# Router copies, slot tables and norm factors placed elsewhere, and the last tail's roots taken together

## What is computed

```
x_lat = x_lat + mod_l[2] * o_lat                       # mixer, gated
h_lat = _modulate(_rmsnorm(x_lat, norm_ffn[l]), mod_l[3], mod_l[4])
...
g_logits = h @ w_group + b_group ; grp = argmax(g_logits)      # 4 groups
e_logits = (h @ w_expert + b_expert)[grp]                       # 8 experts of the group
top_p, top_i = top_k(softmax(e_logits), 2)
y = sum over the two experts of gate * (silu(x @ w1[e]) * (x @ w3[e])) @ w2[e]
x_lat = x_lat + mod_l[5] * y
...
return _rmsnorm(x_lat, final_norm)                     # then the second block starts with its own rmsnorm
```

## Time and profile before

| | |
|---|---|
| median of 3 runs | 2405.39 us (2403.98 to 2409.56) |
| the profiled execution, its own time | 2406.93 us |
| its span | 2405.6 us |
| TensorE busy (matmul) | 2192.5 us, 91% of the span |
| VectorE, ScalarE, GpSimd busy | 657.5, 357.0, 121.5 us |
| read from HBM, written | 589.84 MB, 21.23 MB |

### The profile page before, as it was taken

How to read it: one execution, slowest core, us unless ns; L and a number is a source line. 1 busy time by engine, 2 the same in 40 slices (tenths; PEclk the granted TensorE clock), 3 DMA queues, 4 the chain that set the end, 5 groups by cost and what they waited for, 6 DMA issues and landing times. The chain is left out here.

```text
span 2405.6 us, 27733 instructions
## 1 busy us (share of the span) xinstructions
PE 2192.5 (91%) x11542; PEld 1348.4 (56%) x11542; DVE 657.5 (27%) x1485; ACT 357.0 (15%) x831; POOL 121.5 (5%) x164
## 2 busy tenths in 40 slices
PE   6987998899999986999979999998599999989998
PEld 2454664656665543444555554544376458858873
DVE  2142332422222212313531111111355231034201
ACT  2052431200000001112520000000121122011000
POOL 4000000010000001000000000000110000000000
PEclk9988999899999998899989999999799999999999
DMA  9453163599999997621189999999644432443441
GB/s 331 143 216 136 56 260 149 209 414 420 420 420 420 421 420 295 225 71 67 50 322 415 420 419 420 419 420 418 229 142 134 133 112 97 158 140 119 153 152 41
DMA packets 154309, 601.75 MB, mean 250 GB/s; under 512 B 15289, under 2 KB 19073, under 8 KB 103488
## 3 DMA queue, kind: packets, MB, share of 16 engines
q1 hardware_dynamic: 144512, 582.98, 62.9%
q0 software_dynamic: 8144, 11.57, 1.5%
q10 hardware_dynamic: 1520, 5.32, 0.6%
HBM read 589.84 MB, written 21.23 MB: 254 GB/s over the span
## 5 line engine op out<-in xcount | busy, mean ns | idle before, releaser
L366 PE MATMUL psum<-ring,h_t 128*128 128x512 f32 (+1 forms) x1024 | 430.3, 582 | 4.5 <-ACT h_t L1072 2.1
L366 PEld LDWEIGHTS psum<-ring,h_t 128*128 128x128 f32 x1024 | 192.9, 193 | 234.8 <-issue 230.4
L399 PE MATMUL psum<-h_t,ring 128*128 128x256 f32 (+1 forms) x1424 | 311.7, 382 | 4.5 <-ACT ff_hid L2567 2.3
L399 PEld LDWEIGHTS psum<-h_t,ring 128*128 128x128 f32 (+1 forms) x1424 | 270.0, 190 | 45.9 <-issue 4.7
L2381 PE MATMUL psum<-ring,h_t 128*64 128x256 f32 x2272 | 262.1, 384 | 3.0 <-DMA ring<-in_expert_w_dram 2.1
L2381 PEld LDWEIGHTS psum<-ring,h_t 128*64 128x64 f32 x2272 | 158.0, 137 | 90.3 <-issue 11.8
L2381 PE MATMUL psum<-wide,h_t 128*64 128x256 f32 x1664 | 191.0, 382 | 2.3 <-DMA wide<-in_expert_w_dram 1.5
L2381 PEld LDWEIGHTS psum<-wide,h_t 128*64 128x64 f32 x1664 | 114.9, 137 | 66.6 <-issue 7.6
L337 DVE COPY h_t<-psum 128x512 f32<-128x512 f32 (+2 forms) x76 | 50.4, 663 | 319.6 <-PE psum L1933 294.5
L1933 PE MATMUL psum<-gates,h_row_tiles 128*128 128x256 f32 (+1 forms) x512 | 109.1, 370 | 5.6 <-DVE gates L1921 5.6
L1933 PEld LDWEIGHTS psum<-gates,h_row_tiles 128*128 128x128 f32 x512 | 89.9, 202 | 25.0 <-issue 12.2
(11 more groups left out here) (590 smaller groups left out, 2093.1 us busy)
## 6 DMA issues: line engine op xcount, KB each, us to landing
ring<-in_expert_w_dram SPq DMA_DIRECT2D x210, 1024.0 KB, 24.6
wide<-in_expert_w_dram SPq DMA_DIRECT2D x156, 1024.0 KB, 26.2
ring<-in_ada_w_dram SPq DMA_DIRECT2D x48, 1024.0 KB, 11.3
ring<-in_w_in_dram SPq DMA_DIRECT2D x30, 1024.0 KB, 5.1
ring<-in_diff_w_in_dram SPq DMA_DIRECT2D x12, 1024.0 KB, 15.7
gates<-in_expert_w_dram SPq DMA_DIRECT2D x12, 1024.0 KB
x<-in_expert_w_dram SPq DMA_DIRECT2D x12, 1024.0 KB, 27.8
ring<-in_w_gate_dram SPq DMA_DIRECT2D x12, 1024.0 KB, 4.9
```

The source lines that it names most:

```text
L366: mm = k.nc.tensor.matmul(banks[r][0:m, 0:nn], lhs(k0 + j, r), w[:, j, :], start=(k0 + j == 0), stop=(k0 + j == k_tiles - 1))
L399: mm = k.nc.tensor.matmul(banks[i][0:h, 0:n_rhs], w[:, j, b:b + h], rhs(k0 + j), start=(k0 + j == 0), stop=(k0 + j == k_tiles - 1))
```

## The change

Six edits, cut to their core:

```
 # second_tail: one root for both tiles, on [P, 2] instead of [P, 1] twice
-        def root(i):
+        def roots():
+            t_all, v2_all, r_all = ss[:, 0:T_LAT, 0], ss[:, 0:T_LAT, 1], ss[:, T_LAT:2 * T_LAT, 0]
             wait_for(dve, now(k.act_step, k.dve_step))
...
-        root(0)
         times_g(1)
-        r_at = reciprocal(0)
         squares(1, x[:, 1, :], v2_of(1), D ** -0.5)
         k.dve_step.mark(nc.vector.tensor_tensor_reduce(... accum_out=t_of(1)))
-        for half in range(2):
-            scale(0, half, r_at)
-        root(1)
-        for kt in range(DK):
-            turn(0, kt)
-        r_at = reciprocal(1)
...
+        r_at = roots()
+        for i in range(T_LAT):
+            for half in range(2):
+                scale(i, half, r_at)
+        for i in range(T_LAT):
+            for kt in range(DK):
+                turn(i, kt)

 # route: table of group 0 right behind at_slot, inside the read-out of the counts
-            nc.vector.scalar_tensor_tensor(out=picks.at[:], in0=rank, ...)
+            chain(nc.vector, k.dve_step, nc.vector.scalar_tensor_tensor(out=picks.at[:], in0=rank, ...))
+            picks.select(0)
...
         nc.vector.wait_ge(k.dve_evac.sem, k.dve_evac.n)
-        picks.select(0)
+        ranked = now(k.dve_evac)
...
 # route: next norm factors and the table of group 1 ahead of the slot tables
+        between()
         picks.first_group(rows_at)
+        table_bank = k.psum[:, 5, :]
+        def slot_tables():
+            wait_for(nc.tensor, told_at)
+            for mm in tokens_to_slots(nc.tensor, [table_bank]):
+                k.tensor_done.mark(mm)
+            return now(k.tensor_done)
+        nc.vector.wait_ge(k.tensor_done.sem, picks.picked[0, 3])
+        picks.select(1)
+        wait_for(nc.tensor, ranked)
         picks.first_up()
-        wait_for(nc.tensor, told_at)
...
+        wait_for(nc.vector, slot_tables())
         k.dve_evac.mark(to_tables(table_bank))

 # experts: the gates' copies behind norm_to_columns instead of ahead of it; between() leaves this place
-        k.behind("pool", k.stage())
-        for a in ffn_gates:
-            k.pool_step.mark(nc.gpsimd.tensor_copy(a[SLOT:P, 0:BANK], a[SLOT:P, BANK:D]))
...
         norm_to_columns(k, f"ffn{l}", ...)
+        k.behind("pool", k.stage())
+        for a in ffn_gates:
+            k.pool_step.mark(nc.gpsimd.tensor_copy(a[SLOT:P, 0:BANK], a[SLOT:P, BANK:D]))
...
         routed = k.stage()
-        between()

 # first_tail: scaled rows of tiles 0 and 1 ahead of the first sum of tile 2
+    parts = scaled_rows(0)
     add_pair(2)
-    turn(0, scaled_rows(0))
+    turn(0, parts)

 # first_blocks: leaves VectorE's queue here
-        dve.wait_ge(*last_of(0))
-        picks.select(1)
```

More of the change, by code:

```diff
@@ L1162, in squares @@
             k.act_step.mark(nc.scalar.activation(junk[:], src, ACT.Square, scale=scale, accum_out=to))
-        def root(i):
+        def roots():
+            t_all, v2_all, r_all = ss[:, 0:T_LAT, 0], ss[:, 0:T_LAT, 1], ss[:, T_LAT:2 * T_LAT, 0]
             wait_for(dve, now(k.act_step, k.dve_step))
-            chain(dve, k.dve_step, nc.vector.tensor_scalar(t_of(i), t_of(i), 1.0 / D, eps, ALU.mult, ALU.add))
-            k.dve_step.mark(nc.vector.scalar_tensor_tensor(out=r_of(i), in0=t_of(i), scalar=eps, in1=v2_of(i),
+            chain(dve, k.dve_step, nc.vector.tensor_scalar(t_all, t_all, 1.0 / D, eps, ALU.mult, ALU.add))
+            k.dve_step.mark(nc.vector.scalar_tensor_tensor(out=r_all, in0=t_all, scalar=eps, in1=v2_all,
                                                            op0=ALU.mult, op1=ALU.add))
             wait_for(act, now(k.dve_step))
-            k.act_step.mark(nc.scalar.activation(r_of(i), r_of(i), ACT.Sqrt))
-        def reciprocal(i):
+            k.act_step.mark(nc.scalar.activation(r_all, r_all, ACT.Sqrt))
             wait_for(dve, now(k.act_step))
-            k.dve_step.mark(nc.vector.reciprocal(r_of(i), r_of(i)))
+            k.dve_step.mark(nc.vector.reciprocal(r_all, r_all))
             return now(k.dve_step)
@@ L1658, in scalar_phase, with route @@
     k.pump()
-def route(k, l, h_t, n_tiles, tables, rows, h_rows, gather_from, send_to, slot_w, control, n_blocks, picks, place_room, slot_w_lat):
+def route(k, l, h_t, n_tiles, tables, rows, h_rows, gather_from, send_to, slot_w, control, n_blocks, picks, place_room, slot_w_lat,
+          between):
     nc, sb = k.nc, k.sb
@@ L1781, in ranks @@
             rank = bank[:, 0:32 * n].rearrange("p (i e) -> p i e", e=32)
-            nc.vector.scalar_tensor_tensor(out=picks.at[:], in0=rank, scalar=1.0, in1=chosen[:, 0:n, :], op0=ALU.add,
-                                           op1=ALU.mult)
+            chain(nc.vector, k.dve_step, nc.vector.scalar_tensor_tensor(
+                out=picks.at[:], in0=rank, scalar=1.0, in1=chosen[:, 0:n, :], op0=ALU.add, op1=ALU.mult))
+            picks.select(0)
             nc.vector.tensor_scalar(extra[:, 0, :], bank[:, 32 * n:32 * n + 32], -(SLOT + 1) / 2, 1.0 / SLOT, ALU.add,
@@ L1879, in route @@
         control_at = (k.dve_step.sem, k.dve_step.n)
+        between()
         picks.first_group(rows_at)
-        picks.first_up()
-        wait_for(nc.tensor, told_at)
[L1884 to L1887, removed]
+        table_bank = k.psum[:, 5, :]
[7 more added lines that the diff above has]
+        wait_for(nc.tensor, ranked)
+        picks.first_up()
+        wait_for(nc.vector, slot_tables())
         k.dve_evac.mark(to_tables(table_bank))
@@ L2020, in experts @@
         slot_w_lat = sb(f"slot_w_lat{l}", [P, n_blocks], where=moe) if l == 0 else None
-        k.behind("pool", k.stage())
-        for a in ffn_gates:
-            k.pool_step.mark(nc.gpsimd.tensor_copy(a[SLOT:P, 0:BANK], a[SLOT:P, BANK:D]))
-        gates_at = now(k.pool_step)
         gates_of = [a[:, 0:BANK] for a in ffn_gates]
@@ L2050, in experts @@
                         [rows[:, i, :] for i in range(n_tiles)], tables["router_w"])
+        k.behind("pool", k.stage())
+        for a in ffn_gates:
+            k.pool_step.mark(nc.gpsimd.tensor_copy(a[SLOT:P, 0:BANK], a[SLOT:P, BANK:D]))
+        gates_at = now(k.pool_step)
         k.pump_to = k.taken + 6 * 32
         h_stored, control_at = route(k, l, h_t, n_tiles, tables, rows, h_rows, gather_from, send_to, slot_w, control,
-                                     n_blocks, picks, y_room[:, 0:256 * n_tiles], slot_w_lat)
+                                     n_blocks, picks, y_room[:, 0:256 * n_tiles], slot_w_lat, between)
         if picks.fetched:
```

## The result

The change made the kernel faster by about twice what was forecast: 2385.15 us median of 4 runs (2381.86 to 2393.94) against 2405.76 of before, a ratio of 0.9923 with a 95% interval of 0.9894 to 0.9952. Forecast were 2396.3 and 2393.0 to 2402.0. Two later sets of six runs gave ratios of 0.9919 (0.9897 to 0.9942) and 0.9924 (0.9898 to 0.9950). The mean of all 16 runs of the changed kernel, the four above among them, is 2386.6 us; that of the 75 runs of the kernel before that were taken beside the experiments is 2403.7 (2393.9 to 2411.9): 17.1 +- 2.5 us, where my sum gave 9.1. (In this document +- is twice the standard error of the means.)

What follows compares the result with a forecast made beforehand. The prediction took expert stages as bound by when weights begin streaming without gaps, set by TensorE freeing slots. Gains of 5.2 (layer 0), 3.1 (layer 1) and 0.8 (tail) sum to 9.1 us: 2396.3 us, range 2393.0 to 2402.0.

Steps and rivals of the forecast that it cites:

- Gates' copies: Router norm: 1.89 us leave the root but return ahead of the logits' copy; taken as 0, 0.4 us either way.
- Rival (c): Routing: moved copies lengthen TensorE's pause behind the logits, 1.2 GHz holds through the picks; 8.9 us slower, 2414.3; chance 0.04.
- The size in layer 0: Layer 0's routing: slots come free 5.7 us sooner, less 0.5 for the fetch, so 5.2 us gained.
- clock term: Slow 1.2 GHz work behind the removed pause returns to full speed: 1.34 us in layer 0, 1.69 in layer 1.
- the fetch: Layer 0: GpSimd's fetch of rows now lies beside the weights; charged 0.5 us (0 to 1.2).
- Table of group 1: Written before the slot tables, it removes TensorE's pauses; with the clock, 5.26 us in layer 0, 3.25 in layer 1.
- rival (a): The clock falls all the same, so 1.34 and 1.69 us are not won: 6.1 us gained, 2399.3; chance 0.29.
- The weights follow: Expert stages: slots freed sooner start the weight stream sooner, since gaps of 7.0 and 3.4 us leave room.
- rival (b): Transfers alone set the weight stream, TensorE waits longer at the stage's end: 1.5 us gained, 2403.9; chance 0.12.
- Layer 1: Layer 1's routing: shift of 3.55 us, room 3.4 of which some 0.3 stay empty; 3.1 us gained.
- Second tail: Tail of layer 1: the last copy out ends sooner, 0.8 us gained (0.3 to 1.3).
- tail of layer 0: Root may come 0.6 us sooner, but TensorE then waits for weights anyway: 0, at most 0.6 us.

Runs made afterwards that it cites:

- e10: The changed kernel ended behind layer 0's experts, the rest of the program left out; mean of five 938.5 us, against 948.8 for the kernel before ended there.
- e11: The kernel before with only the gates' copies moved behind the router norm, run whole for a second trace; one run, 2401.5 us.
- e3: The kernel before with only the second tail's roots in one; 2399.1 us (12 runs), 4.6 +- 3.4 us faster.
- e9: The kernel before, ended behind layer 0's experts with the rest left out; mean of five 948.8 us.
- e13: The kernel before, ended behind layer 1's experts with what follows left out; 1702.5 us.
- ended kernels: Changed kernel against the kernel before, both ended behind layer 0's experts (938.5 against 948.8 us) or layer 1's (1688.0 against 1702.5 us).

## Why the prediction was wrong

- **The step that failed: "Gates' copies ... I take 0".** The waits moved as the prediction said, though the two sides don't quite cancel: the root won 1.6 us (TensorE's pause ahead of the transposes 6.11 instead of 7.70) and the logits' copy lost 1.31 (TensorE's wait 2.06 instead of 0.75). But the step priced the moved wait by its length alone, and it also moves TensorE's 1.2 GHz stretch, from the picks of group 0 onto the turning back, where VectorE ends last anyway. With moved and waited-for copies the turning back took 5.3 to 5.4 us in nine of ten traces and 3.71 in the tenth (e10); in the ten others it took 3.71 every time. The picks took 7.38 to 7.41 us in eight of the ten, 9.0 in e10 and e11; in the seven traces of the old order 9.0 or 10.3. To the first pick of group 1 the copies alone win 2.7 us (44.0, mean of three traces, instead of 46.7), to the end of the experts 3.9. Rival (c) had this very mechanism and gave it the other sign. How much of this reaches the time is not shown: the whole kernel with the copies alone gained 1.5 +- 1.9 us.
- **The size in layer 0.** From the last sum to the first pick of group 1 it is 39.7 us (mean of five traces) instead of 46.7 (four: before, e3, e9, e13): 7.0, of which the pause with its wake-up is 4.1, and 2.9 are the router, the table of group 0 and the picks' clock. From there to the turn of the last experts' rows it is 470.4 instead of 473.5 us: 3.1, where my clock term less the fetch was 0.8. Together 10.1, and 10.3 +- 4.6 by the ended kernels, against 5.2.
- **Table of group 1.** Right in mechanism: no pause, 1.98 us, 3.67 us in layer 1. The clock term was right in cause, and in layer 1 in size (1.69 in every trace). In layer 0 it was too small: 1.34 was read from one of the two mildest of nine traces, whose mean is 2.2. Whole kernels put this edit, in both layers, at 11.1 +- 4.4 alone and 10.0 +- 3.4 among the others; my steps said 7.6 and 7. So the copies are not the only term that was short. The prediction put 0.29 on rival (a), that the clock falls all the same. There the Trainium skill (TensorE: Matmul & The Clock Gate, "What's actually happening") was cited for a monitor that runs freely. That the same pause might therefore cost no stretch in some runs was my own step from it. Here it cost one in 9 of 9, in layer 1 in 6 of 6; what differed was its length.
- **The weights follow** (rival (b) fell): what layer 0's routing won is there at the end of its experts. The 0.5 us charged for the fetch is not to be seen.
- **Layer 1.** 4.3 us between the two ends (14.6 - 10.3), +- 7, for 3.1. The traces agree in size, 2.6 us by their means: 29.2 to 29.9 us instead of 30.8 to 31.4 from the last sum to the picks of group 1, and from there to the start of the tail 463.9 to 468.2 (three traces) instead of 465.6 to 468.4 (six with the old order of the table).
- **Second tail.** 0.9 to 1.2 us in the seven traces that have this edit and nothing else new in the tail, for 0.8 (0.3 to 1.3). It does not explain the 4.6 +- 3.4 of its own runs. The tail of layer 0, put at 0, shows nothing either: from the last product of its experts to the last square sum of layer 1's router norm it is 261.4 to 264.8 us in eight traces with that edit, 261.2 to 264.4 in seven without.
- **What stays open.** By the traces these sum to about 14 us (10.1, 2.6 and 1.1), with the 14.6 of the ended kernels for both layers to 15.7; the runs say 17.1 +- 2.5. The whole kernel with the copies alone gained 1.5 +- 1.9, less than the 3.9 us that the traces of this edit show by the end of layer 0's experts; I did not find where they go. By the whole kernels the excess would lie with the table (some 3 us) and the last tail (some 4), by the traces with the copies and the clock behind the pause; the errors allow both. And why the slow stretches come where they do, ahead of the router above all, was not tried.

No version beat the changed kernel by what can be told: 2387.7 (own semaphore, 12 runs) and 2384.8 (pauses filled), against 2386.6.

## What to carry to other kernels

A wait that is only moved need not be worth nothing when TensorE runs in short bursts around it: look at which instructions run at 1.2 GHz, whether they or the work beside them have slack, and onto which ones the stretch falls when the pause ahead of them changes. Price each pause taken out by its length and by the slow products right behind it, and take those from more than one trace: here they cost 1.4 to 2.8 us behind the same pause. And before a forecast of a few thousandths take the scatter from more than three runs: three of this kernel lay within 6 us, 75 within 18.

## What the runs showed of the hardware that I had not expected

- The granted clock can be raised by useless products (0.966 to 0.971 in the mean, 3.41 to 1.96 us for the tail's transposes), yet the time hardly follows (1.8 +- 3.8 us), though over the runs of one kernel time and clock go together.
- One and the same program reaches the same instruction at 401.77 or 408.61 us.
- A 128x128 product of f32 by f32 stands as two instructions of some 0.12 us each in the trace: 24 of them took 5.55 us (x48).
